# Mixer projections of a two-layer trunk: from one float32 product to three rounded products, with the remainders subtracted on GpSimd

## What is computed

```python
def _mixer(x, st, p, l):
    u = x @ p['w_in'][l] + p['b_in'][l]               # 1024 -> 7320 columns, 58 tiles of 128 in the kernel
    (rw, mqk, mv, mo, mi, mf, gq, gk, gv, gg, ga, rx, ry, gates) = _split(u, IN_SIZES)
    ...   # four recurrent branches: RWKV7, mLSTM, GLA, RG-LRU
    branches = jnp.stack([o_a, o_b, o_c, o_d], axis=2)
    up = jnp.einsum('blgc,gcd->blgd', branches, p['w_branch'][l])
    gate = jax.nn.sigmoid(gates.reshape(B, L, N_BRANCH, D))
    merged = jnp.einsum('blgd,blgd->bld', gate, up)
    return merged @ p['w_out'][l], ...

def _trunk(x, states, p):
    for l in range(DEPTH):                            # DEPTH = 2
        m_out, st_new = _mixer(x, st, p, l)
        x = _layer_norm(DN_ALPHA * x + m_out, ...)
        f = _swiglu(x, ...) if l % 2 == 0 else _moe(x, ...)   # 8 experts, 2 per token
        x = _layer_norm(DN_ALPHA * x + f, ...)
```

## Time and profile before

| | |
|---|---|
| median of 3 executions | 1970.82 us (1970.04 to 1975.36) |
| the profiled execution | 1969.92 us |
| its span in the profile | 1968.1 us |
| TensorE matmul busy | 1852.4 us, 94% |
| VectorE / ScalarE / GpSimd busy | 1255.4 / 834.0 / 15.3 us |
| mean granted TensorE clock | 0.963 |

### The profile page before, as it was taken

One profiled execution on the slowest core, in us unless ns is written; L12 is line 12 of the kernel. 1 busy time (PEld: TensorE's weight loads), 2 busy tenths in 40 slices (PEclk: granted clock), 3 DMA queues, 4 the chain that ended last, 5 costly groups with the idle time before them and its releaser, 6 DMA issues.

```text
span 1968.1 us, 24319 instructions
## 1 busy us (share of the span) xinstructions
PE 1852.4 (94%) x9310; PEld 1517.5 (77%) x9310; DVE 1255.4 (64%) x1507; ACT 834.0 (42%) x856; POOL 15.3 (1%) x32
## 2 busy tenths in 40 slices
PE   8999999979998999999995999999899999999896
PEld 6777788879997867778874877777687877777685
DVE  2656634146643436753326887889798978888794
ACT  1222112133332312311103666666666656766673
POOL 1000000000001000000000000000000000000000
PEclk9999999989998979999995999999999999999999
DMA  8330222535553423311214897988798988989770
GB/s 345 120 103 19 119 108 77 181 129 174 191 192 101 135 70 106 124 68 51 109 49 186 306 351 272 338 323 336 276 342 319 342 300 317 344 319 343 278 299 22
DMA packets 59290, 402.71 MB, mean 205 GB/s; under 512 B 8672, under 2 KB 9344, under 8 KB 11312
## 3 DMA queue, kind: packets, MB, share of 16 engines
q1 hardware_dynamic: 54144, 393.80, 53.8%
q0 software_dynamic: 1600, 3.97, 0.6%
q10 hardware_dynamic: 3440, 3.41, 0.5%
HBM read 396.67 MB, written 4.49 MB: 204 GB/s over the span
## 4 chain that ended last, share of the span: by engine, by line
PE 50%; DVE 2%; ACT 2%; issue 2%; DVEq 0%; ACTq 0%
PE mA L1813 30%; PE mW L1813 19%; ACT WH L642 1%; PE mA L1742 1%; ACT X L917 0%; DVE HEL L1091 0%; DVE ring_low L969 0%; DVE V L1611 0%; DVE XEL L1059 0%; PE mW L1695 0%; DVE SQ L1613 0%; DVE SQ L1605 0%; DVE XTL L976 0%; PE mW L1714 0%; ACT V L910 0%
## 5 line engine op out<-in xcount | busy, mean ns | idle before, releaser
L969 DVE TENSOR_TENSOR ring_low<-ring,WH 128x2048 fp32r<-128x2048 f32 x192 | 438.4, 2290 | 82.5 <-ACT WH L642 81.3
L1813 PE MATMUL mA<-X,ring 128*128 128x264 f32 x1664 | 397.0, 393 | 17.7 <-DMA ring<-in_w_in_dram 9.4
L642 ACT ACTIVATE WH<-ring 128x2048 fp32r<-128x2048 f32 x188 | 359.1, 1913 | 66.7 <-PE mW L1813 56.2
L1813 PEld LDWEIGHTS mA<-X,ring 128*128 128x128 f32 x1664 | 316.5, 193 | 80.6 <-issue 17.0
L1813 PE MATMUL mA<-WH,XEH 128*128 128x512 f32 x704 | 295.0, 419 | 9.0 <-DVE XEL L1059 7.6
L1813 PE MATMUL mA<-WH,XEL 128*128 128x512 f32 x704 | 279.7, 397 | 0.0
L1813 PE MATMUL mA<-ring_low,XEH 128*128 128x512 f32 x544 | 216.7, 398 | 0.0
L969 DVE TENSOR_TENSOR more_low<-more_ring,WH 128x2048 fp32r<-128x2048 f32 x72 | 164.9, 2290 | 23.3 <-ACT WH L642 23.0
L1813 PEld LDWEIGHTS mA<-WH,XEH 128*128 128x128 f32 x704 | 134.2, 191 | 40.5 <-DVE ring_low L969 11.3
L1813 PEld LDWEIGHTS mA<-WH,XEL 128*128 128x128 f32 x704 | 134.0, 190 | 31.7
L642 ACT ACTIVATE WH<-more_ring 128x2048 fp32r<-128x2048 f32 x72 | 137.7, 1912 | 24.5 <-PE mW L1813 21.0
(11 more groups left out here) (386 smaller groups left out, 2809.7 us busy)
## 6 DMA issues: line engine op xcount, KB each, us to landing
ring<-in_moe_dram SPq DMA_DIRECT2D x192, 1024.0 KB, 4.8
more_ring<-in_moe_dram SPq DMA_DIRECT2D x72, 1024.0 KB, 4.9
ring<-in_w_in_dram SPq DMA_DIRECT2D x52, 1024.0 KB, 6.2
ring<-in_ffn_up_dram SPq DMA_DIRECT2D x20, 1024.0 KB, 4.8
ring<-in_ffn_down_dram SPq DMA_DIRECT2D x11, 1024.0 KB, 4.8
ring<-in_w_branch_dram SPq DMA_DIRECT2D x7, 1024.0 KB, 5.0
RTAIL<-in_w_in_dram SPq DMA_DIRECT2D x6, 1024.0 KB, 5.3
ring<-in_w_out_dram SPq DMA_DIRECT2D x6, 1024.0 KB, 9.1
```

Source lines behind the costliest of these rows:

```text
L642: nact.activation(WH[:, HI_SLOT[j % PAIR], :], expert_slot(j), ACT.Copy).then_inc(weights_hi, 1)
L969: v.tensor_tensor(expert_low(j), expert_slot(j), WH[:, HI_SLOT[j % PAIR], :].bitcast(F32), SUB)\
L1813: return nc.tensor.matmul(out, w, x, start=start, stop=stop, skip_group_check=True)
```

## The change

The `w_in` pairs of the mixers, but for the first two of each layer (`PLAIN`), are computed with three rounded products. ScalarE rounds each slot in two halves, as steps of its stream, one or two pairs ahead (`HI_AHEAD`); GpSimd subtracts in two halves and writes the remainder over the raw weight; TensorE does 48 float32r instructions for a pair in place of 16 float32 products. `X` is rounded by ScalarE and split by VectorE once a layer ahead of the mixer. `w_out`, `w_branch` and the first two pairs stay as they are. The raw weights have four slots, the rounded ones two (and for the first ones two more places in `MG` and `GT`, while these are unused), the `up` weights one. The three state loads move from GpSimd's queue to ScalarE's. The up products trail their gates by one pair. The FFN rounds three slots ahead and writes its remainders in place. The fill tables are written anew for the finer steps.

```diff
-SLOTS = 9
-MSLOTS = 8
+SLOTS = 7
+MSLOTS = 9
...
+PAIRS = [item for item in STREAM if item[0] != "up"]
+PLAIN = 2
+HI_PLACE = [0, 1, "mg", "gt", 0, 1, "mg", "gt", 0, 1, "gt", "mg"] + [0, 1] * 8
+HI_AHEAD = [2] * 14 + [1] * 13
+RAW = ((0, 1, 2, 3), (3, 4, 5, 6))
+HI_SLOTS = ((4, 5), (0, 1))
+UP_SLOT = (6, 2)
+FF_SLOTS = (4, 5, 6, 0, 1, 2, 3)
...
-PE_FILL = {"loads9": 18, "rg.conv": 41, "ml.qk": 87, "ml.logd0": 4, "ml.kw3": 3, "ml.abs": 3, "ml.h": 12,
+PE_FILL = {"loads9": 24, "rg.conv": 95, "ml.qk": 312, "ml.logd0": 13, "ml.kw3": 9, "ml.abs": 6, "ml.h": 43,
...
@@ gpsimd
-                pool.wait_ge(*dve_of.at("rg.out", l))
-                pool.dma_start(MS, A["mC"][l]).then_inc(layer_in, 16)
-                pool.wait_ge(*dve_of.at("ml.out", l))
-                pool.wait_ge(*pe_of.at("ml.c", l))
-                pool.wait_ge(state_out, 16 * (12 * l + 7))
-                pool.dma_start(GS, A["gS"][l]).then_inc(layer_in, 16)
-                pool.wait_ge(*dve_of.at("gl.out", l))
-                pool.wait_ge(state_out, 16 * (12 * l + 9))
-                pool.dma_start(DS, A["rS"][l]).then_inc(layer_in, 16)
+                for split in range(PLAIN, len(PAIRS)):
+                    w = of_pair[l, split]
+                    for half in range(2):
+                        pool.wait_ge(*w.hi(half))
+                        nc.gpsimd.tensor_tensor(halves_of(w.low, half), halves_of(w.raw, half),
+                                                halves_of(w.rounded, half).bitcast(F32), ALU.subtract).then_inc(lo_done, 1)
...
@@ scalar
+            act.wait_ge(x_in, 16)
+            for half in range(2):
+                round_x(half)
...
+                    for n, item in enumerate(PAIRS):
+                        while split < len(PAIRS) - PLAIN and split + PLAIN <= n + HI_AHEAD[split]:
+                            w = of_pair[l, PLAIN + split]
+                            act.wait_ge(*w.landed)
+                            if w.place_freed:
+                                act.wait_ge(*w.place_freed)
+                            for half in range(2):
+                                nact.activation(halves_of(w.rounded, half), halves_of(w.raw, half), ACT.Copy).then_inc(hi_done, 1)
+                                yield
+                            split += 1
...
                 fill("ml.conv")
+                act.wait_ge(*dve_of.at("rg.out", l))
+                act.dma_start(MS, A["mC"][l]).then_inc(state_in, 16)
...
                 fill("gl.cum")
+                act.wait_ge(*pe_of.at("ml.c", l))
+                act.wait_ge(state_out, 16 * (12 * l + 7))
+                act.dma_start(GS, A["gS"][l]).then_inc(state_in, 16)
...
+                act.wait_ge(*dve_of.at("gl.out", l))
+                act.wait_ge(state_out, 16 * (12 * l + 9))
+                act.dma_start(DS, A["rS"][l]).then_inc(state_in, 16)
                 fill("rw.mixed")
...
@@ vector
+                for h in range(2):
+                    split_x(2 * l, h)
                 fill("loads9")
...
@@ tensor
+            def split_tile(kind, l, i, w, q, name):
+                free(numbers[kind, l, i])
+                wh, wl = (x.rearrange("p (k n) -> p k n", k=KT)[:, :, P * q:P * q + P] for x in (w.rounded, w.low))
+                for k in range(KT):
+                    if q == 0 and k % 4 == 0:
+                        pe.wait_ge(*w.lo(k // 4))
+                    for a, x in ((wh, XH), (wh, XL), (wl, XH)):
+                        ins = mm(acc(kind, l, i), a[:, k, :], x[:, k, :], ...)
+                        yield
```

More of the change, by code:

```diff
@@ L65, with streamed_work @@
[L65 to L71, removed]
+def streamed_work():
+    seq = [("u", i) for i in (TMI - 1, TRX, TRY, TMQ, TMK, TMV, TMO, TGQ, TGV, TGG, TR, TK, TV)]
+    late = []
+    for g in (RG, ML, GL, RW):
+        for q in range(4):
+            seq.append(("gate", g, q))
+            late.append(("up", g, q))
+            if len(late) > 1 and late[0][1] != RW:
+                seq.append(late.pop(0))
+    return seq + late
@@ L475, in program, with __init__, hi, lo @@
         HT, ETH = ar(2, 256), ar(2, 256)
-        chunks = []
+        weights, last_user, landings, splits = [], {}, [0] * SLOTS, [0]
+        class Weight:
+            def __init__(self, source, slot, user, place=None):
+                self.source, self.slot, self.user = source, slot, user
+                self.freed = last_user.get(slot)
+                last_user[slot] = user
+                landings[slot] += 1
+                self.landed = slot_in[slot], 16 * landings[slot]
+                self.raw, self.low = slots[:, slot, :], slots_rounded[:, slot, :]
+                if place is not None:
+                    self.rounded, key = place
+                    self.place_freed = last_user.get(key)
+                    last_user[key] = user
+                    self.split = splits[0]
+                    splits[0] += 1
+                weights.append(self)
+            def hi(self, half):
+                return hi_done, 2 * self.split + half + 1
+            def lo(self, half):
+                return lo_done, 2 * self.split + half + 1
@@ new lines, in hi_place, with ffn_used @@
+        def hi_place(l, s):
+            p = HI_PLACE[s]
+            if p == "mg":
+                return mg_rounded[:, :], ("mg", l)
+            if p == "gt":
+                return gt_rounded[:, :], ("gt", l)
+            return slots_rounded[:, HI_SLOTS[l][p], :], HI_SLOTS[l][p]
+        def ffn_used(i):
+            p, w = divmod(i - 2 * FC, 3)
+            if p >= 0 and w == 2:
+                return pe_of.at("ff.down", 0, 2 * p + 1)
+            return pe_of.at("ff.part", 0, i - max(p, 0))
@@ new lines, in program @@
+                place = hi_place(l, n - PLAIN) if n >= PLAIN else None
+                of_pair[l, n] = Weight(source, RAW[l][n % 4], user, place)
+                if item in (PAIRS[NU // 2 - 1], ("gate", ML, 3), ("gate", GL, 3), ("gate", RW, 3)):
+                    g = item[1] if item[0] == "gate" else RG
+                    ups = KT * (RG, ML, GL, RW).index(g)
+                    of_up[l, g] = Weight(A["w_branch"][l, g], UP_SLOT[l], pe_of.at("mg.up", l, ups + KT - 1))
+            for p in range(4):
+                of_out[l, p] = Weight(A["w_out"][l, p], RAW[l][(len(PAIRS) + p) % 4], pe_of.at("mg.out", l, 2 * p + 1))
@@ L500, in landed, with halves_of @@
+            if l == 0:
+                for i in range(2 * FC + 12):
+                    source = A["ffn_up"][i] if i < 2 * FC else A["ffn_down"][i - 2 * FC]
+                    of_ffn.append(Weight(source, FF_SLOTS[i % SLOTS], ffn_used(i), (FWH[:, i % 4, :], ("ffn", i % 4))))
+        uses0 = landings + [0] * (XSLOTS - SLOTS)
+        def halves_of(ap, half):
+            return ap[:, SLOT // 2 * half:SLOT // 2 * half + SLOT // 2]
         def landed(m, j):
@@ L529, in _ @@
             sp.dma_start(X[:, :, :], A["x"]).then_inc(x_in, 16)
-            for i, (src, _) in enumerate(chunks):
-                if i >= SLOTS:
-                    sp.wait_ge(*chunks[i - SLOTS][1])
-                sp.dma_start(ring_slot(i % SLOTS), src).then_inc(slot_in[i % SLOTS], 16)
+            for i, w in enumerate(weights):
+                if w.freed:
+                    sp.wait_ge(*w.freed)
+                sp.dma_start(w.raw, w.source).then_inc(slot_in[w.slot], 16)
                 if i == 1:
@@ L2198, in _ @@
                 for p in range(4):
-                    for _ in pair("out", "mg.out", l, 2 * p, [MG[:, k, :] for k in range(KT)]):
+                    for _ in plain_pair("out", "mg.out", l, 2 * p, of_out[l, p], [MG[:, k, :] for k in range(KT)]):
                         pass
```

226 lines of the change are left out of this document (113 added, 113 removed), and 8 rows, old and new, of the table PE_FILL.

## The result

| | before | after |
|---|---|---|
| median, us | 1973.09 (1970.04 to 1979.29, 4 executions) | 2054.11 (2052.63 to 2055.01, 4 executions) |
| ratio | | 1.0401, 95% interval 1.0379 to 1.0424 |
| profiled execution, span | 1969.92, 1968.1 | 2054.3, 2052.5 |

The kernel became slower by 81 us, where 1915 was forecast and 2005 was the upper end. The head and the busy times of the page of after stand against the earlier trace rows; the share line is its chain of waits, the last three lines GpSimd's new groups.

What follows compares the result with a forecast made beforehand. TensorE's instructions were taken to bound the mixers. Cheaper products save 70 us, terms against it cost 7 us a layer, 14 in all, so 56 off gives 1914, or 1915 as median; own range 1900 to 1932, all cases 1900 to 2005.

Steps and rivals of the forecast that it cites:

- the steps: TensorE's mixer work per layer falls from 235.0 to 199.9 us: 17.3 along the chain, 17.8 in the rest behind it.
- the price of a product: On TensorE, 0.445 us in float32 becomes 0.364 as three float32r instructions; 0.081 saved on each of 864, 70 us.
- the shortened fills: Some thirty points of the mixer lose 0.1 to 0.7 us of fill; 0.13 us new waiting each, 4 us a layer.
- ScalarE's 2 us: Rounding 27 slots a layer delays chain operations or the emptying of tiles on ScalarE: 2 us a layer, bounds 0 and 10.
- the end of the chain: Gates left to cover the last 9.2 us shrink from 28 to 10.2 us: cost 1 us a layer, bounds 0 and 4.
- X: Two roundings and two subtractions of X a layer, ahead of or beside other work: zero, or 2.3 us if uncovered.
- the loads: Weight loads stay covered by the four raw slots; state loads moved to ScalarE take under 2 us inside its idle time.
- the 2.9 that decides: GpSimd time per half, in us, at which a pair's two halves take as long as its 5.8 us of TensorE work.
- costs TensorE nothing by its length: GpSimd's 54 halves of 2.1 us, 113 us in some 370 a layer, run one to two pairs ahead, so TensorE never waits.
- The rival that had such a term: GpSimd's subtractions block VectorE's operations on two SBUF operands in the mixers: 40 us a layer, 1995 us; chance 0.35.
- Its first term: Stretch up to the end of `ml.qk`: 13 halves, 0.75 of them meeting VectorE, 2.1 us each, 20 us a layer.
- Its second term: The other 41 halves, 36 in the chain: half of them meet VectorE at 1.1 us each, 20 us a layer.

Runs made afterwards that it cites:

- the tiny run: The changed kernel with GpSimd subtracting only 2 of 1024 columns of each half, the third product taking the rounded weight instead: 1919.42 us, ratio 0.9727.
- the run with 8 pieces: The changed kernel with each half subtracted by GpSimd in 8 instructions of 128 columns instead of one of 1024: 1998.89 us, ratio 1.0129.

## Why the prediction was wrong

*The gain was right.* With GpSimd nearly out of the way the kernel takes 1919 against a forecast of 1915. In the traces (the tiny run's profiled execution is its fastest, 1913.3) layer 0 ends 28.7 us earlier (404.3 to 375.6) and both layers 56.6 (1968.1 to 1911.5), where 28 and 56 were worked out. Of layer 0's, 9.6 come before the chain's end (342.8 to 333.2), where the steps gave 17.3 - 7 = 10.3, and 19.1 behind it, where they gave 17.8. So the price of a product, the shortened fills, ScalarE's 2 us, the end of the chain, X and the loads held together as sums; the loads of the states were run alone and are 0. The place of each of the 7 us was not measured.

*The step that failed is GpSimd.* Its length was sized well enough, 2.1 us estimated against 2.50 to 2.58, below the 2.9 that decides. The Trainium skill (GPSIMD Engine Reference, Elementwise — side-by-side cycle accounting) gives 4497 ns for 2048 elements; the estimate from it, 2.25 for a half, was nearer: the 12 halves that met no operation of VectorE took 2.37, and the mean lies a tenth above 2.25 since halves are held too. Waits of TensorE for GpSimd are single, 3.1 us in the first mixer. What failed is the step "costs TensorE nothing by its length": the forecast's sum had no term for what GpSimd does to VectorE's chain. That term measures 67 us a layer, 135 together or 1.25 for each half, and it alone turns a gain of 54 us into a loss of 81. The rival that had such a term was the right one.

*The rival's mechanism was right and its size was not.* It gave 40 us a layer and 1995; measured are 67, and 2054. Its first term held: 20 us up to the end of `ml.qk`, measured 24.1 in layer 0 (6.2 of them before 50 us, which it had not counted) and 17.8 in layer 1. Its second term was mis-sized: 20 us for all other halves, measured 45.7 (69.8 - 24.1). It had 36 halves in the chain and half of them meet VectorE, at 1.1 us, so 0.55 each. But 26 of the 36 lie between L1308 and L1533, where much of the chain is on SBUF: VectorE is held 1.1 us by each of them there and the kernel loses 1.6 to 1.7 (41.7 and 44.3 us), while the 10 beside the RWKV chain, which reads much from `mW`, cost at most 0.4. What the kernel loses there beyond VectorE's own time goes with the clock, where "some us" was too little: TensorE spends 20 us more on the same instructions, at 0.83 in place of 0.92. How much of the loss the clock makes by itself was not separated.

*The chances.* Against the rival the prediction held that nothing in the trace showed the two engines to share anything. That was no evidence, since GpSimd computed nothing in that trace. The rule that was cited (the Trainium skill, SBUF — State Buffer, Who interferes with whom) speaks of just this pair, and every run here agrees with it: a two-operand operation of VectorE is held by a subtraction or a copy and not by a memset (0.71 us against 2.79 and 1.42). The 0.35 for that rival should have been the larger share. And the range ended at 2005, where the rival's bound, every half at its full length wherever VectorE is busy, would have given 54 x 0.75 x 2.1 = 85 us a layer, 2085.

*The marks for the next profile* were the right ones: TensorE's busy share in the mixer fell to 86% in place of over 95%, VectorE's SBUF groups were longer with those on `mW` unchanged, and TensorE waited 11 us in the fill of `ml.qk`, though under ScalarE's name. GpSimd's 136 us in a mixer were above the 110 to 125.

## What to carry to other kernels

Work given to an idle GpSimd is not free if it reads SBUF while VectorE runs a chain on two SBUF operands: price each of its instructions at up to its full length wherever that chain is what others wait for (here 1.2 to 1.8 of 2.5 us), and at next to nothing where VectorE reads PSUM or waits. If such work must be there, put it in those places or cut it into small instructions, even if GpSimd then takes 1.7 times as long, and look in the trace for an operation that is held over a whole run of them. And give a rotation of buffers that two engines fill in turn one place more than the steady state needs, since a single wait of TensorE can be paid again in its clock.

## What the runs showed of the hardware

- A VectorE operation on 16 or 18 columns takes 2.3 us beside a GpSimd subtraction of 2.5 us, where it took 0.15 to 0.18: the hold does not depend on its size.
- A GpSimd instruction that only writes (1.8 us) leaves two-operand operations of VectorE alone, but holds its one-operand scalar operations on SBUF (0.44 became 2.09 us).
- On GpSimd 128x1024 takes 2.50 to 2.58 us to subtract and 1.14 to copy, and a subtraction of 128x2 takes 0.20 to 0.34 (means of groups).
- The hold goes both ways: GpSimd's copies take between 1.04 and 1.61 us from 44 to 84 us, the long ones beside VectorE's two-operand operations. Its subtractions take 2.33 to 3.41 us in the changed kernel, and those that met no operation of VectorE 2.37.
- Short GpSimd instructions that follow each other without a gap can hold one VectorE operation through all of them: 10.7 us over 26 pieces of 0.46 us, in the run with 8 pieces.
